# Moving a split weight ring by 128 bytes and the split tiles of x and y by 64 bytes in a decoder layer

## What is computed

```python
h = rms_norm(x, norm_pre_g)
q_a, k_a, v_a, g_a, f_a, q_b, k_b, v_b, g_b = split(h @ w_in)      # 4*512 + 8 + 4*512 columns
log_f = log_sigmoid(f_a + fox_forget_b)
y_a = fox_attention(q_a, k_a, v_a, log_f) * silu(g_a)     # logits + F[t] - F[s], causal
y_b = moba_attention(q_b, k_b, v_b, slopes) * silu(g_b)   # logits - slope * distance, causal
return x + rms_norm(concat(y_a, y_b) @ w_out, norm_post_g)
```

## Time and profile before

| what | value |
|---|---|
| median of three runs | 145.1 us (145.02 to 145.14) |
| profiled execution, its time | 145.13 us |
| profiled execution, its span in the trace | 143.3 us |
| TensorE matmul | 134.4 us busy, 1076 instructions |
| TensorE weight load | 127.4 us busy, 1076 instructions |
| VectorE | 109.4 us busy, 230 instructions |
| ScalarE | 98.7 us busy, 198 instructions |
| GpSimd | 40.0 us busy, 58 instructions |
| mean granted clock of TensorE | 0.992 of full speed |

### The profile page before, as it was taken

The page is one execution under the profiler, slowest core; times in us unless marked ns, Lnnn a source line. Parts: engine busy times, 40 slices in busy tenths (PEclk is TensorE's granted clock), DMA queues, the critical chain, the costliest instruction groups (busy, mean ns, idle before and its releaser), DMA issues.

```text
span 143.3 us, 2857 instructions
## 1 busy us (share of the span) xinstructions
PE 134.4 (94%) x1076; PEld 127.4 (89%) x1076; DVE 109.4 (76%) x230; ACT 98.7 (69%) x198; POOL 40.0 (28%) x58
## 2 busy tenths in 40 slices
PE   7789999999999999999999999999999999999910
PEld 7679999999999999999999999999998888988910
DVE  0384966899999999988888977999689816471891
ACT  4376989678976398977875977778879833355740
POOL 3621100000000067000599235230735551120042
PEclk9999999999999999999999999999999999999996
DMA  4999999398865999758368603449600000000034
GB/s 110 233 313 386 401 395 342 88 375 254 271 223 172 389 392 377 278 160 238 112 230 237 213 9 142 146 166 293 280 2 0 0 0 5 0 0 0 0 149 146
DMA packets 9725, 26.96 MB, mean 188 GB/s; under 512 B 1384, under 2 KB 2416, under 8 KB 9456
## 3 DMA queue, kind: packets, MB, share of 16 engines
q1 hardware_dynamic: 9120, 25.57, 52.0%
q10 hardware_dynamic: 592, 1.22, 2.3%
HBM read 25.73 MB, written 1.06 MB: 187 GB/s over the span
## 4 chain that ended last, share of the span: by engine, by line
PE 87%; DMA 4%; issue 2%; DVE 2%; ACT 1%; POOL 1%; SPq 1%; POOLq 1%; DVEq 0%; ACTq 0%
PE bank L937 47%; PE score_banks L947 11%; PE bank L1128 7%; PE score_banks L1128 5%; PE score_banks L1033 4%; PE value_banks L947 4%; DMA raw<-in_w_units 4%; PE value_banks L1056 1%; PE value_banks L1044 1%; PE value_banks L1060 1%; PE value_banks L1045 1%; POOL x_t L366 1%; DVE h L882 1%; PE bank L1046 1%; PE value_banks L1059 1%
## 5 line engine op out<-in xcount | busy, mean ns | idle before, releaser
L615 DVE TENSOR_TENSOR w_lo<-raw,w_hi 128x1024 fp32r<-128x1024 f32 (+1 forms) x33 | 44.6, 1353 | 6.6 <-ACT w_hi L380 6.5
L380 ACT ACTIVATE w_hi<-raw 128x1024 fp32r<-128x1024 f32 (+1 forms) x33 | 34.4, 1056 | 6.5 <-DMA raw<-in_w_units 4.1
L937 PE MATMUL bank<-h_hi,w_hi 128*128 128x256 f32 x128 | 36.0, 281 | 0.0
L937 PE MATMUL bank<-h_lo,w_hi 128*128 128x256 f32 x128 | 35.6, 278 | 0.0
L937 PE MATMUL bank<-h_hi,w_lo 128*128 128x256 f32 x128 | 35.5, 278 | 0.0
L937 PEld LDWEIGHTS bank<-h_hi,w_hi 128*128 128x128 f32 x128 | 24.1, 188 | 0.4
L937 PEld LDWEIGHTS bank<-h_lo,w_hi 128*128 128x128 f32 x128 | 24.0, 188 | 0.0
L937 PEld LDWEIGHTS bank<-h_hi,w_lo 128*128 128x128 f32 x128 | 24.0, 188 | 0.0
L334 POOL TENSOR_TENSOR probs<-probs,row_inv 128x256 f32<-128x256 f32 (+1 forms) x16 | 15.7, 1005 | 27.6 <-DVE row_inv L764 27.5
L937 PE MATMUL bank<-xg_hi,w_hi 128*128 128x256 f32 x64 | 17.8, 278 | 0.0
L937 PE MATMUL bank<-xg_lo,w_hi 128*128 128x256 f32 x64 | 17.7, 277 | 0.0
(11 more groups left out here) (172 smaller groups left out, 326.5 us busy)
## 6 DMA issues: line engine op xcount, KB each, us to landing
raw<-in_w_units SPq DMA_DIRECT2D x30, 512.0 KB, 4.8
raw<-in_w_out SPq DMA_DIRECT2D x4, 512.0 KB, 3.2
h<-in_x SPq DMA_DIRECT2D x2, 512.0 KB, 8.1
y_parts<-in_w_out SPq DMA_DIRECT2D x2, 512.0 KB, 5.6
gpost_row<-in_w_out SPq DMA_DIRECT2D x2, 512.0 KB, 6.1
squares<-decay_rows_scratch ACTq DMA_DIRECT2D x1, 1024.0 KB, 5.9
x_t<-in_x SPq DMA_DIRECT2D x1, 1024.0 KB, 7.1
raw<-in_w_units SPq DMA_DIRECT2D x3, 256.0 KB, 5.2
```

The costliest lines, as they stand in the source:

```text
L380: nc.scalar.activation(w[0][:, s, 0:width], raw[:, s, 0:width], ACT.Copy).then_inc(s_hi, 1)
L615: nc.vector.tensor_tensor(w[1][:, s, 0:width], raw[:, s, 0:width], w[0][:, s, 0:width].bitcast(F32), ALU.subtract).then_inc(s_lo, 1)
L937: last = nc.tensor.matmul(dst, stationary(a, j), moving(b, j), start=n == 1, stop=n == count * len(PASSES))
```

## The change

Four unused tiles are declared. One of 64 bytes per partition stands ahead of the two tiles of `xg` and one of 192 bytes behind them; one of 128 bytes stands ahead of the two tiles of `w` and one of 128 bytes behind them. So all that stands behind `xg` lies 256 bytes further on, and all that stands behind `w` 512 bytes further on, which leaves it where it was modulo 256. No instruction, wait, queue or size is changed.

```diff
+LINE = 64
+X_SHIFT = 16
+RING_SHIFT = 32
...
         x_t = sb("x_t", [P, KT, SEQ])
+        sb("x_shift", [P, X_SHIFT])
         xg = [sb(f"xg_{n}", [P, KT, SEQ], F32R) for n in PARTS]
+        sb("x_shift_back", [P, LINE - X_SHIFT])
         h32 = sb("h32", [P, KT, SEQ])
...
         raw = sb("raw", [P, RING, V_PITCH])
+        sb("ring_shift", [P, RING_SHIFT])
         w = [sb(f"w_{n}", [P, RING, V_PITCH], F32R) for n in PARTS]
+        sb("ring_shift_back", [P, LINE - RING_SHIFT])
         wo = [sb(f"wo_{n}", [P, OUT_OWN, D_MODEL], F32R) for n in PARTS]
```

## The result

The changed kernel takes 146.0 us at the median of six runs (145.70 to 146.36), the kernel before 145.0 us (144.68 to 145.14). The ratio is 1.0052, with a 95% interval from 1.0029 to 1.0075. Its profiled execution took 145.70 us with a span of 143.9 us, 0.6 us longer than that of the kernel before. Forecast were 144.6 us and a gain. All ratios here leave out executions more than 1.5% above the fastest of the same kernel, among them one of the changed kernel at 760.9 us.

The account below looks back on a forecast made before the run. TensorE was taken to bound the kernel through distances between matmul starts. 145.13 us minus 0.50 for keys and query 6, with gates, values, output and other engines at 0, gave 144.6 us; range 143.3 to 146.1 us.

Parts of the forecast that it names:

- What bounds it: From 7.8 to about 132 us TensorE without waits; time is the sum of distances between starts of matmuls.
- Does an address matter: Value units differ by ring slot, 0.01 to 0.02 us or 0.5%: weak evidence that operand placement has a real effect.
- placement is indifferent: Rival: placement changes nothing or swaps equal things, the slow rate comes from the break; 145.1 us, chance 0.22.
- Keys: Five key units after scores or values recover within about 5 products, query 6 starts in step; gain 0.50 us.
- Gates: Eight gate units, 192 products, distance from 64/192 to 128/0: taken as 0, bounds 0 to +0.84 us.
- Queries: Query units get the alignment where the slow rate persists, but follow gates or keys directly, so begin at the fast rate.
- The other engines: ScalarE, VectorE and DMA: effect 0; TensorE can be 0.5 us earlier at the transposes without a new wait.
- Values: Eight value units, distance from 64/192 to 128/0: taken as 0, up to 0.16 us either way, 1.0 us room downwards.
- Output: Output projection, 72 products of 512 columns and 48 of 256: taken as 0, room 0.67 and 0.21 us, loss 0.53.
- The rival of the bad distance: Gates lock into the slow rate, +0.84 us, output loses +0.53; 146.0 us with the keys' gain, 146.5 without; chance 0.21.

Follow-up runs that it names:

- x_only: Kernel before with only the split tiles of x and y moved 64 bytes, the weight ring at its old place; ratio 1.0058 (1.0034 to 1.0081).
- low_64: Kernel before with only the low half of the weight ring moved 64 bytes further on; ratio 1.0119 (1.004 to 1.0198).
- pitch_1088: Kernel before with a ring slot of 1088 floats instead of 1056, so all slots are at distance 64; ratio 0.9978 (0.9945 to 1.0012).
- ring_x_128: Kernel before with the weight ring and the split tiles of x and y both 128 bytes further on; ratio 0.9964 (0.9937 to 0.999), repeated 0.998 (0.9944 to 1.0017).
- ring_256: Kernel before with the weight ring and all behind it 256 bytes further on; ratio 0.9982 (0.9949 to 1.0015).
- ring_16: Kernel before with the weight ring 16 bytes further on, distances 80 and 208; ratio 1.011 (1.0035 to 1.0186).

## Why the prediction was wrong, point by point

- **What bounds it** held, but for one short wait in both kernels that the prediction didn't see (below). The other engines' least durations are the same (line 615, now 622: 1194 ns against 1193), and the whole change lies in the distances between products.
- **Does an address matter**: yes, by more than the earlier trace rows let one see. x_only changes nothing but an address and costs 1.06 us in the chain. The Trainium skill, "TensorE: Matmul & The Clock Gate", section "Step-by-step: what each phase is for", says that loading the next weights takes no read bandwidth from the running matmul. What the prediction drew from it, that placement is indifferent, did not come out for these fp32r products. Whether the rule itself fails isn't shown: that it is the two reads that meet is my reading, and low_64, which should have shown it, didn't.
- **Keys** was right in mechanism and size. Forecast was a gain of 0.50 us, five stretches gave 0.54. Behind their first product the keys had two slow distances and not five. But the gain of the last one, 0.08 us, was taken back by the wait below, so 0.46 us came through. The explanation by slot is to be put as the distance of 64, as pitch_1088 shows.
- **Gates** is the step that failed. I took 0, since 64 and 192 have the same rate, and from two equal values inferred that the rate is flat in between. It isn't: 0 and 128 have 120.0 and 118.3 ns. The term put at nothing measured +1.09 us, more than the whole gain of the keys. The upper bound was too low as well, because I priced it at the slow rate that a row showed (117.7 ns, +0.84 us), while there are two slower ones. From the first gate product to the first query it took 22.02 us before and 23.11 after: +1.09 us.
- **Queries** were to begin in step, since each follows a gate or a key with nothing between. Query 0 didn't: it ran at 117.8 ns, and with key 0, which recovered, that is +0.12 us. Whether the slow gates handed this on stays open, since query 0 of ring_x_128 did the same behind gates in step.
- **The other engines: a wait.** The transposes behind the last key wait for VectorE. They write the bank that its sum of line 787 (794 in the changed kernel) reads, and line 1039 waits for it. The two instructions of that sum, first in the kernel before (the transpose is in the earlier trace rows), then in the changed one:

```profile
105.28 1.41 DVE L787 TENSOR_TENSOR y_parts<-value_banks,y_parts 64x512 f32<-64x512 f32 x2 [0.47 <-ACT y_parts L484]
```

```profile
105.84 1.41 DVE L794 TENSOR_TENSOR y_parts<-value_banks,y_parts 64x512 f32<-64x512 f32 x2 [0.70 <-ACT y_parts L491]
```

  The last product of the key before them, then the first transpose, in the changed kernel's timeline:

```profile
107.08 0.28 PE L944 MATMUL bank<-h_hi,w_lo 128*128 128x256 f32 x1
107.35 0.30 PE L1051 MATMUL value_banks<-ident,probs 128*128 128x128 f32 x1
```

  The sum ends at 106.69 us in the kernel before and at 107.25 in the changed one, and the first transpose starts 0.10 us later both times, as it does in the profiles of all these runs. So the wait isn't new. It hid in 0.19 us between the last key product and the transpose, and with a faster key it became 0.27 us, +0.08. I had read 1.5 us of cover off GpSimd's probabilities, which was the wrong input: VectorE left no cover at all.
- **Values** was right at 0: from 14.96 to 29.53 us before and from 14.76 to 29.34 after, +0.01 us. The four units of the earlier trace rows changed by -0.02, +0.04, -0.02 and +0.03 us, those in odd slots (now 0) down and those in even slots (now 128) up.
- **Output** was right at 0, +0.04 us. Here is the row that answers to the second of the earlier trace rows; both ends of my bounds (-0.88 and +0.53 us) were far off.

```profile
113.39 2.72 PE score_banks L1135 x12
```

The sum as it came: gates +1.09, keys and query 6 -0.54, query 0 and key 0 +0.12, the wait +0.08, values and output +0.05: +0.80 us. The rival of the bad distance gave 146.0 us, the time measured, but in part by luck: its gates were too cheap (+0.84 us at a rate that they didn't have), and its output term of 0.53 us did not come.

Of the versions tried ring_x_128 has the shortest chain, 0.23 us less than the kernel before in line 937, and 0.15 and 0.07 us less from the first gate product to the last product of the output in its two profiles (106.83 and 106.91 against 106.98). Its first interval lies below 1, its second holds 1, so a gain of 0.1 to 0.2 us is likely and not shown.

## What to carry to other kernels

Where TensorE alone bounds a kernel, read the distance between starts of matmuls by unit, not their mean duration: two or more rates for one shape are worth as much as a wait. The placement of the two operands to each other is then a size of its own to measure, over its whole period: two good values say nothing of those between them. And a slow rate can outlive what started it, so look at how each stage is entered and at hitches of under 0.1 us. A gain ahead of a wait is worth only what the wait leaves: look for every input of the instruction behind it, also for who still reads the bank that it writes.

## What the runs showed of the hardware that I had not expected

- For products of 256 columns in fp32r with a weight load of 128 columns each, at the full clock, the distance between starts is 113.3 ns (in step) or 117.8 (out of step) at operand distances of 64 and 192 bytes modulo 256, 118.3 to 118.4 at 128, 120.0 at 0, and 116.5 to 118.9 at 80, 96, 208 and 224.
- Out of step is a state that lasts: 0.07 us lost at one product was followed by three slow units, 0.35 us in all (ring_256), and in pitch_1088 it lasted from 29 to 66 us. No unit came back into step at a distance of 192; at 64 most did, but not all.
- In the three placements profiled twice the sums of the chain repeat to 0.01 us. From the first gate product to the last of the output it is 106.98 us twice and 107.78 us twice, but 106.83 and 106.91 for ring_x_128. The start of the first gate product varies by up to 1.2 us between profiles (29.07 to 30.24 us).
- Products that alternate between 512, 256 and 264 columns (the values) and those of 512 and 256 in the output hardly react to the change: +0.01 us of 14.6 and +0.04 of 26.7. In ring_16 the output took 27.00 us, 0.28 more than before. Why was not tried.
